# Output products of two pairs side by side in the mixers of a two-block transformer kernel

## What is computed

```
q = (h @ w_q).reshape(B, S, N_HEADS, HEAD_DIM).transpose(0, 2, 1, 3)
...
causal = (own * MOBA_BLOCK + jnp.arange(MOBA_BLOCK))[None, :] <= t[:, None]
s_own = jnp.where(causal, s_own, -jnp.inf)
p = jax.nn.softmax(jnp.concatenate([s_sel, s_own], axis=-1), axis=-1).astype(qc.dtype)
...
return out @ w_o
```

## Time and profile before

| | us |
|---|---|
| three runs, median (lowest to highest) | 1855.36 (1855.32 to 1855.46) |
| profiled execution | 1855.36 |
| its span in the profile | 1853.5 |
| TensorE busy in the span | 1843.1 |
| VectorE, ScalarE busy | 1208.5, 990.5 |

### The profile page before, as it was taken

The page is one execution under the profiler, slowest core; times in us unless marked ns, Lnnn a source line. Parts: engine busy times, 40 slices in busy tenths (PEclk is TensorE's granted clock), DMA queues, the critical chain, the costliest instruction groups (busy, mean ns, idle before and its releaser), DMA issues.

```text
span 1853.5 us, 26785 instructions
## 1 busy us (share of the span) xinstructions
PE 1843.1 (99%) x9601; PEld 1544.6 (83%) x9601; DVE 1208.5 (65%) x1491; ACT 990.5 (53%) x1297; POOL 160.6 (9%) x260
## 2 busy tenths in 40 slices
PE   9999999999999999999999999999999999999998
PEld 8878888888877888888888887788888888878887
DVE  7875665668876665667755647656666556576555
ACT  6774554456775464445544556644454444575443
POOL 8110010002210010000100031000020000100000
PEclk9999999999999999999999999999999999999999
DMA  8346556655435466555656554465565555535553
GB/s 275 106 148 207 173 194 203 204 182 154 155 127 189 168 203 204 194 181 181 205 186 204 179 194 138 154 204 192 178 200 184 184 194 194 181 114 175 182 187 114
DMA packets 204724, 333.18 MB, mean 180 GB/s; under 512 B 10976, under 2 KB 149856, under 8 KB 204640
## 3 DMA queue, kind: packets, MB, share of 16 engines
q1 hardware_dynamic: 201376, 320.82, 52.0%
q0 software_dynamic: 3120, 11.02, 1.8%
q10 hardware_dynamic: 144, 0.26, 0.0%
HBM read 331.01 MB, written 1.05 MB: 179 GB/s over the span
## 4 chain that ended last, share of the span: by engine, by line
PE 95%; POOL 2%; DVE 1%; issue 1%; ACT 1%; DMA 0%; POOLq 0%; ACTq 0%; DVEq 0%
PE ps L828 21%; PE ps L669 18%; PE ps L638 18%; PE ps L647 18%; PE ps L846 11%; PE ps L707 3%; PE ps L939 2%; PE ps L951 2%; PE ps L967 2%; POOL stat L2784 0%; ACT whi L1494 0%; DMA prob<-start_dram 0%; POOL mask L2834 0%; POOL stat L2783 0%; POOL hid L2956 0%
## 5 line engine op out<-in xcount | busy, mean ns | idle before, releaser
L2020 DVE TENSOR_TENSOR wlo<-raw,whi 128x2048 fp32r<-128x2048 f32 (+1 forms) x294 | 664.2, 2260 | 180.3 <-ACT whi L1494 176.6
L1494 ACT ACTIVATE whi<-raw 128x2048 fp32r<-128x2048 f32 (+3 forms) x306 | 569.4, 1861 | 133.8 <-PE ps L647 132.0
L828 PE MATMUL ps<-act,whi 128*128 128x512 f32 x1728 | 403.6, 390 | 0.0
L828 PEld LDWEIGHTS ps<-act,whi 128*128 128x128 f32 x1728 | 323.5, 188 | 66.6
L1557 ACT ACTIVATE hid<-ps 128x512 f32<-128x512 f32 x54 | 32.2, 597 | 396.2 <-PE ps L846 396.2
L2092 DVE TENSOR_TENSOR hid<-ps,hid 128x512 f32<-128x512 f32 x54 | 37.3, 692 | 314.2 <-ACT hid L1557 314.2
L846 PEld LDWEIGHTS ps<-act,wlo 128*128 128x128 f32 x1728 | 214.5, 192 | 4.2
L846 PE MATMUL ps<-act,wlo 128*128 128x256 f32 x1728 | 215.8, 283 | 0.0
L638 PE MATMUL ps<-wlo,act 128*128 128x512 f32 (+2 forms) x768 | 207.4, 385 | 0.0
L669 PE MATMUL ps<-whi,act 128*128 128x512 f32 (+2 forms) x760 | 201.9, 386 | 0.1
L647 PE MATMUL ps<-whi,act 128*128 128x512 f32 (+2 forms) x760 | 198.6, 381 | 0.0
(11 more groups left out here) (272 smaller groups left out, 1951.2 us busy)
## 6 DMA issues: line engine op xcount, KB each, us to landing
raw<-ffn_w_gate_dram SPq DMA_DIRECT2D x88, 512.0 KB, 4.0
raw<-ffn_w_up_dram SPq DMA_DIRECT2D x88, 512.0 KB, 4.9
raw<-ffn_w_down_dram SPq DMA_DIRECT2D x88, 512.0 KB, 4.3
raw<-w_in_dram SPq DMA_DIRECT2D x62, 512.0 KB, 4.5
raw<-w_ffn_gate_dram SPq DMA_DIRECT2D x44, 512.0 KB, 4.0
raw<-w_ffn_up_dram SPq DMA_DIRECT2D x44, 512.0 KB, 5.0
raw<-w_ffn_down_dram SPq DMA_DIRECT2D x44, 512.0 KB, 4.4
raw<-a_w_qkv_dram SPq DMA_DIRECT2D x24, 512.0 KB, 4.4
```

What stands on the lines that cost most here:

```text
L828: nc.tensor.matmul(ps[:, 2 * g + j, :], vh[:, k, g, j * P:(j + 1) * P], both[:, 4 * half + k, :, :], start=half == 0 and k == 0, stop=False)
L1494: nc.scalar.activation(whi[:, u % SLOTS, half:words], raw[:, u % SLOTS, half:words], ACT.Copy)\
L2020: nc.vector.tensor_tensor(wlo[:, u % SLOTS, 0:words], raw[:, u % SLOTS, 0:words], whi[:, u % SLOTS, 0:words].bitcast(F32), ALU.subtract)\
```

## The change

Only block 2's mixers change. A table CAUSAL_AT says at which step which pairs' output products stand: pair 0 at step 3 as before, pairs 1 and 2 at step 7, 3 and 4 at 11, 5 and 6 at 15, pair 7 behind the last turn. Bank 3 takes two pairs, in its two halves (causal_place), and four heads' turned probabilities live, so the copies go to probT and probT_more in turn. ScalarE's high halves and VectorE's low halves of two pairs stand side by side too, and wait for the later of the two (last_beside). Output block 0 stays at steps 4 and 5; block p from 1 to 4 moves from steps 2p + 4 and 2p + 5 to 2p + 6 and 2p + 7, and blocks 5 and 6 stand around and behind the last products. The steps at which ScalarE and VectorE split weights stay as they are.

```diff
+CAUSAL_AT = {3: (0,), 7: (1, 2), 11: (3, 4), 15: (5, 6), 17: (7,)}
...
-        def probs_place(sc, causal):
-
-            if causal:
-                return probT[:, sc % 2]
+        def probs_place(sc):
+
             return probT[:, sc % 4] if sc % 4 < 2 else probT_more[:, sc % 4 - 2]
+
+        def last_beside(pair):
+
+            together = [both for both in CAUSAL_AT.values() if pair % (H2 // 2) in both][0]
+            return pair - pair % (H2 // 2) + together[-1]
+
+        def causal_place(pair):
+
+            return slice(pair % 2 * S, (pair % 2 + 1) * S)
...
-                    if not odd and causal and pair % (H2 // 2):
+                    if not odd and causal and pair % (H2 // 2) and sc % H2 // 2 in starts:
                         was_read("pair", pair - 1)
...
-                    if s % 2 and s >= 3:
-                        outputs(heads[s - 3], heads[s - 2])
+                    if s in CAUSAL_AT:
+                        outputs(*heads[2 * CAUSAL_AT[s][0]:2 * CAUSAL_AT[s][-1] + 2])
...
-                others.update({2 * p + 4 + t: lambda p=p, t=t: output_block(p, pair, (t,))
-                               for p in range(last - 1) for t in range(T)})
+                others.update({(2 * p + 6 if p else 4) + t: lambda p=p, t=t: output_block(p, pair, (t,))
+                               for p in range(last - 2) for t in range(T)})
                 attend(heads, values, others)
                 heads[-1].turn()
-                output_block(last - 1, pair, (0,))
+                output_block(last - 2, pair, (0,))
                 outputs(heads[-2], heads[-1])
-                output_block(last - 1, pair, (1,))
+                output_block(last - 2, pair, (1,))
+                output_block(last - 1, pair)
...
-                    if s >= 2 and s % 2:
-                        pair = (s - 2) // 2
+                    for pair in CAUSAL_AT.get(s, ()):
                         pair_hi((sc // 2) + pair, o2_hi[:, pair, :])
...
-                    if s >= 4 and s % 2 == 0:
-
-                        pair = (s - 3) // 2
+                    for pair in CAUSAL_AT.get(s - 1, ()):
                         pair_lo(sc // 2 + pair, o2_lo[:, pair, :], o2_hi[:, pair, :])
```

More of the change, by code:

```diff
@@ L955, in head @@
                 pair, odd = sc // 2, sc % 2
+                starts = [together[0] for together in CAUSAL_AT.values()]
                 def output_bank():
@@ L965, in output @@
                     c0 = kt * P if causal else 0
-                    o = ps[VD * odd:VD * (odd + 1), 3 if causal else 5 + 2 * (pair % 2), c0:S]
-                    return nc.tensor.matmul(o, v[:, kt], probs_place(sc, causal)[:, kt, c0:S],
+                    rows_ = slice(VD * odd, VD * (odd + 1))
+                    o = ps[rows_, 3, causal_place(pair)] if causal else ps[rows_, 5 + 2 * (pair % 2), 0:S]
+                    return nc.tensor.matmul(o[:, c0:S], v[:, kt], probs_place(sc)[:, kt, c0:S],
                                             start=kt == 0, stop=kt == T - 1)
@@ L1619, in probs_turned @@
                 if causal:
-                    nc.scalar.activation(probs_place(sc, True)[:, 0, :], bank[:, 0, :], ACT.Copy)
-                    nc.scalar.activation(probs_place(sc, True)[:, 1, P:S], bank[:, 1, P:S], ACT.Copy)\
+                    nc.scalar.activation(probs_place(sc)[:, 0, :], bank[:, 0, :], ACT.Copy)
+                    nc.scalar.activation(probs_place(sc)[:, 1, P:S], bank[:, 1, P:S], ACT.Copy)\
                         .then_inc(sem("turn_read_a"), 1)
                 else:
-                    nc.scalar.activation(probs_place(sc, False), bank, ACT.Copy).then_inc(sem("turn_read_a"), 1)
+                    nc.scalar.activation(probs_place(sc), bank, ACT.Copy).then_inc(sem("turn_read_a"), 1)
             def pair_hi(pair, dst):
-                act.wait_ge(sem("pair_done"), w.at("pair_done", pair + 1))
-                src = ps[:, 3 if w.layer is None else 5 + 2 * (pair % 2), 0:S]
+                last = last_beside(pair) if w.layer is None else pair
+                act.wait_ge(sem("pair_done"), w.at("pair_done", last + 1))
+                src = ps[:, 3, causal_place(pair)] if w.layer is None else ps[:, 5 + 2 * (pair % 2), 0:S]
                 nc.scalar.activation(dst, src, ACT.Copy).then_inc(sem("pair_hi"), 1)
@@ L2201, in pair_lo @@
             def pair_lo(pair, dst, hi):
-                dve.wait_ge(sem("pair_hi"), w.at("pair_hi", pair + 1))
-                src = ps[:, 3 if w.layer is None else 5 + 2 * (pair % 2), 0:S]
+                dve.wait_ge(sem("pair_hi"), w.at("pair_hi", (last_beside(pair) if w.layer is None else pair) + 1))
+                src = ps[:, 3, causal_place(pair)] if w.layer is None else ps[:, 5 + 2 * (pair % 2), 0:S]
                 rest(dst, src, hi).then_inc(sem("pair_read_v"), 1)
```

## The result

The changed kernel takes **1886.43 us** (median of 4 runs, 1885.05 to 1887.5); the kernel before, run beside it, 1855.41 (1855.32 to 1855.46). The ratio is 1.0167, 95% interval 1.0155 to 1.0179: 31.0 us slower, by far more than a measurement can miss. The direction was forecast, the size was not: 1875.9 was said, and the range ended at 1883.0. The profiled execution took 1887.5 us, 32.1 more than that of before (1855.36).

What follows compares the result with a forecast made beforehand. TensorE, busy 99% of the span, was taken as the bound. Idle 10.6 us less 0.5 saved plus 0.2 behind the mixer gave 10.3 a mixer, 20.5 in two, on 1855.36: 1875.9 us, range 1871.5 to 1883.

Steps and rivals of the forecast that it cites:

- products: Products of pairs 1 and 2, after scores of heads 8 and 9: wait for copies of head 5, 0.21 us idle.
- turn 5: Turn of head 5: TensorE waits for ScalarE's copies of the previous turn, which share one bank; 0.40 us idle.
- turn 7: Turn of head 7: waits for its normalise behind VectorE's 2.20 us weight split; 1.40 us idle.
- block(1,0): First output tile of pair 1: waits for the low half of pair 1 on VectorE; 0.66 us idle.
- turns 9 and 13: Turns of heads 9 and 13: exponentials stand behind ScalarE splits waiting for moved output blocks; 3.84 us idle each.
- last block: End of the mixer: ScalarE's split in halves at step 16 waits for block(5,1); 0.24 us idle.
- a block's border: Border between an output block and another kind of step: 0.10 us each, two fewer, 0.2 us saved a mixer.
- Rival (a): TensorE's clock falls to half rate in the new gaps, some 3.4 us lost each; 1882.5 to 1889 us; chance 0.12.
- all four: The clock falls in all four 3.7 us gaps of the two mixers: 1889 us.
- (b): Only steps 5 to 8 wait, 2.67 us idle a mixer; 1859.7 us; chance 0.06.
- (c): Not slower: only the shorter steps count, 1854.4 us, 1853 at the bound; chance 0.04.
- the split at step 8: ScalarE's weight split waits about 3.5 us for block(1,1), ahead of exponentials 9; 3.84 us idle before turn 9.

Runs made afterwards that it cites:

- filled gaps: Changed kernel plus 38 transposes of the identity into an unread bank ahead of turns 9 and 13; 1878.19 us.
- blocks in twos: Kernel before, products one pair at a time, both tiles of most output blocks at one step, weight splits behind the last use of their slots; 1855.06 us.
- only the blocks later: Kernel before with output blocks two heads later and each pair's products still at their own step; 1885.45 us.
- one split later: Changed kernel with only ScalarE's weight split of step 8 moved to step 10, that of step 12 left; 1872.89 us.

## Why the prediction failed, point by point

**What bounds the kernel.** Right: the time is TensorE's steps and its waits. VectorE's and ScalarE's busy time did not change, and the loss is nothing but TensorE idle or slow.

**The waits.** Right, each in its place and with the releaser that was named. From start to start, less the step's own price: products 0.06 (0.91 less 0.85; walked 0.21), turn 5 0.37 (0.84 less 0.47; walked 0.40), turn 7 1.44 (1.75 less 0.31; 1.40), block(1,0) 0.56 (0.80 less 0.24; 0.66), turns 9 and 13 3.98 each (4.44 less 0.46; 3.84), last block 0.33 (0.79 less 0.46; 0.24). Sum 10.7, walked 10.6. Of ScalarE's split it was said that it stands idle for about 3.5 us. It was 4.93 in the changed kernel, as half clock had slowed the work ahead of its release, and 3.40 in the one with filled gaps, at full clock.

**The savings.** Forecast 0.5 a mixer. With the splits moved and no fallen clock, the waits that are left (0.37, 0.06, 1.44, 0.56 twice, 0.33) sum to 3.3 and the mixer grew by 3.06: some 0.25 saved. In the changed kernel itself 10.7 of waits and a rest of 10.4 give about 0.3. So half of the forecast or a little more was saved. Of its terms, the products of two pairs save 0.14 to 0.15, not 0.10; the 0.10 for a block's border came back in the turn where a run could show it (blocks in twos).

**The clock, the step that failed.** The prediction priced the clock and gave it a chance of 0.12, because the gaps of 3.7 us were shorter than the idle time after which the clock was seen to fall at the kernel's end. That row could not bear this: from the last matmul's end at 1846.97 to a clock of 0.50 at 1852, it tells how long one fall took in one place, behind a fully busy stretch. It is no lower bound for another place. In the runs, all ten gaps of 3.81 us (four each in the changed kernel and in the kernel with only the blocks later, two in the one with one split later) had half rate at their end or within 1.2 us of it. Rival (a) was the case: the spells took 11.5 us in the profiled execution, against 4 x 3.4 = 13.6 for "all four" (1889.5, put down as 1889). That these are near is luck in part: there were six spells, two of them behind turn 7, of 1.5 to 2.7 us and not 3.4. The price came from transposes at the kernel's start at 0.26 each; at half clock turn 13 takes 0.52 for three, 0.17 each. The prediction had named the right gaps, and then used the time of one fall in one place as a limit for all.

The Trainium skill (TensorE: Matmul & The Clock Gate, HAM oscillation) says that waits between bursts of matmuls put the clock back again and again. The trace of the changed kernel agrees: six spells in two mixers. The prediction named this page and set it aside against one row of the trace, at the kernel's end.

**The rivals (b) and (c).** Both fell: the split at step 8 does wait, and turns 7 and 9 are late. (b)'s own number has a counterpart: with both splits free, waits at steps 5 to 8 and at block(3,0) remain, 1861.5 measured against 1859.7.

**The range.** It went up to one fallen clock a mixer, 1882.5. There were three a mixer in the profiled execution. Had rival (a) been taken from 1882.5 to 1889 with a weight of one in three, the range would have held the time.

## What to carry to other kernels

Before moving a step later, look for the instruction that waits for its end, and for what stands behind that instruction in its engine's order: here a weight split with nothing urgent about it held up the exponentials of the next head, and two numbers in a list gave back 24.9 of 31.0 us. Where a walk finds gaps of a few us on TensorE, add the price of a fallen clock behind each as the likely case, unless a row of that kernel shows such a gap without it. If a gap can't be removed, matmuls without use can be cheaper than idle time: 152 of them took 8.2 us off this kernel.

## What the runs showed of the hardware

**Gaps much shorter than those at the kernel's end let the clock fall, but not each time.** Behind the gap of 1.2 to 1.7 us before turn 7 it fell in 4 of 10 cases: in both mixers of the changed kernel, in one of two in the kernels with filled gaps and with only the blocks later, and in neither of those with one or both splits moved. In the kernel with both of ScalarE's splits moved, TensorE's work up to there is that of the changed kernel within 0.01 us of idle time (0.20, 1.21, 0.29 against 0.21, 1.20, 0.29), and the clock stayed at 1.00. The six runs of that kernel lie 0.61 us apart, with a mean clock of 0.999 or 1.0 in each, so a spell of 1.5 fits into none of them. What decides it isn't shown by any run, and stays open. In the kernels with long gaps the runs spread more: the changed kernel's lie 2.45 us apart, those of the kernel before 0.14, and one spell costs 1.5 to 2.7; that the spells make this spread is not shown.

**Fewer spells can be worth more than less work.** The kernel with filled gaps has 152 instructions more on TensorE (9753 against 9601), its busy time is 5.4 us longer, and it ends 8.2 us earlier.

**Grouped products tie their readers together.** The copy of one turned head waited for two pairs' products where it had waited for one: 0.72 us before turn 7, seen only after a larger wait in front of it was gone.
